# w2 loads issued from ScalarE's queue instead of SyncE's, in a decoder step with a mixture of experts

## The reference

```python
def _moe(x, router_w, router_b, w1, b1, w2, b2):
    logits = x.astype(jnp.float32) @ router_w.astype(jnp.float32) + router_b.astype(jnp.float32)
    top_logits, top_idx = lax.top_k(logits, TOP_K)
    gates = jax.nn.softmax(top_logits, axis=-1)
    combine = jnp.einsum('tk,tke->te', gates,
                         jax.nn.one_hot(top_idx, N_EXPERTS, dtype=jnp.float32)).astype(x.dtype)
    out = jnp.zeros_like(x)
    for e in range(N_EXPERTS):
        a = x @ w1[e] + b1[e]
        glu = jnp.minimum(a[:, ::2], SWIGLU_LIMIT)
        lin = jnp.clip(a[:, 1::2], -SWIGLU_LIMIT, SWIGLU_LIMIT)
        act = glu * jax.nn.sigmoid(SWIGLU_ALPHA * glu) * (lin + 1)
        out = out + combine[:, e:e + 1] * (act @ w2[e] + b2[e])
    return out
```

## Time and profile before

| | |
|---|---|
| median of three runs | 1176.62 us (1175.73 to 1181.22) |
| profiled execution, its own time | 1177.86 us |
| its span, from the first to the last instruction | 1175.8 us |
| granted TensorE clock, mean | 0.977 of full speed |
| TensorE busy | 1081.0 us |
| ScalarE busy | 165.0 us |
| bytes read from HBM | 428.02 MB |

### The profile page before, as it was taken

How to read it: one execution, slowest core, us unless ns; L and a number is a source line. 1 busy time by engine, 2 the same in 40 slices (tenths; PEclk the granted TensorE clock), 3 DMA queues, 4 the chain that set the end, 5 groups by cost and what they waited for, 6 DMA issues and landing times.

```text
span 1175.8 us, 13859 instructions
## 1 busy us (share of the span) xinstructions
PE 1081.0 (92%) x5783; PEld 503.6 (43%) x5783; DVE 293.6 (25%) x490; ACT 165.0 (14%) x339; POOL 62.9 (5%) x103
## 2 busy tenths in 40 slices
PE   6999999899999999898989998989999999898985
PEld 3567774443434343434343434343434343434332
DVE  5338544622213030303030302030303030202022
ACT  3211112402111010101010101010101010101002
POOL 7007001200000000000000000000000000000000
PEclk9999999898999999999999999999999999999998
DMA  9851139289999999999999999999999999999991
GB/s 339 297 215 28 55 145 327 99 343 404 429 427 426 428 427 429 429 428 430 428 429 428 428 429 428 429 428 428 428 430 429 428 428 428 428 428 427 428 416 42
DMA packets 47684, 432.00 MB, mean 367 GB/s; under 512 B 4919, under 2 KB 13655, under 8 KB 22977
## 3 DMA queue, kind: packets, MB, share of 16 engines
q1 hardware_dynamic: 45472, 428.23, 87.3%
q0 software_dynamic: 752, 2.56, 0.7%
q10 hardware_dynamic: 1424, 0.72, 0.2%
HBM read 428.02 MB, written 3.48 MB: 367 GB/s over the span
## 4 chain that ended last, share of the span: by engine, by line
PE 62%; DMA 31%; DVE 2%; ACT 2%; issue 2%; SPq 1%; POOL 0%; ACTq 0%; DVEq 0%; POOLq 0%
DMA ring<-in_expert_w 31%; PE ps L1560 19%; PE ps L1519 13%; PE ps L1476 7%; PE ps L1459 5%; PE ps L1196 5%; PE ps L1180 4%; PE ps L1329 2%; PE ps L1547 1%; PE ps L1246 1%; PE ps L1262 1%; PE ps L1539 1%; PE ps L1282 1%; SPq L369 1%; DMA ring<-in_meta_tokens 0%
## 5 line engine op out<-in xcount | busy, mean ns | idle before, releaser
L1519 PE MATMUL ps<-ring,mem 128*64 128x512 f32 x2048 | 463.7, 609 | 54.7 <-DMA ring<-in_expert_w 54.3
L1519 PEld LDWEIGHTS ps<-ring,mem 128*64 128x64 f32 x2048 | 160.6, 140 | 350.6 <-issue 349.4
L1560 PE MATMUL ps<-ring,mem 128*64 128x512 f32 x1024 | 224.8, 597 | 5.6 <-ACT mem L707 3.0
L1078 DVE TENSOR_SCALAR mem<-ps 128x512 f32<-128x512 f32 x32 | 22.1, 692 | 708.0 <-PE ps L1519 708.0
L1560 PEld LDWEIGHTS ps<-ring,mem 128*64 128x64 f32 x1024 | 86.6, 138 | 133.0 <-issue 133.0
L700 ACT ACTIVATE mem<-mem 128x512 f32<-128x512 f32 x32 | 20.0, 629 | 482.1 <-DVE mem L1078 482.1
L1476 PE MATMUL ps<-mem 128*128 128x512 f32 (+3 forms) x204 | 79.6, 603 | 3.2 <-DVE mem L1080 1.4
L1459 PEld LDWEIGHTS ps<-mem 128*128 128x128 bf16 x1080 | 60.3, 98 | 12.2 <-issue 12.2
L1196 PE MATMUL ps<-mem,ring 128*128 128x280 f32 x256 | 62.9, 401 | 0.9 <-ACT mem L600 0.9
L1459 PE MATMUL ps<-mem 128*128 128x128 bf16 x1080 | 62.9, 219 | 0.0
L1196 PEld LDWEIGHTS ps<-mem,ring 128*128 128x128 f32 x256 | 47.6, 190 | 13.4 <-issue 2.8
(11 more groups left out here) (258 smaller groups left out, 575.5 us busy)
## 6 DMA issues: line engine op xcount, KB each, us to landing
ring<-in_expert_w SPq DMA_DIRECT2D x192, 2048.0 KB, 25.3
ring<-in_w_in SPq DMA_DIRECT2D x7, 2048.0 KB, 19.9
ring<-in_w_out SPq DMA_DIRECT2D x2, 2048.0 KB, 10.1
ring<-in_state_rec SPq DMA_DIRECT2D x4, 512.0 KB, 10.9
out<-ring SPq DMA_DIRECT2D x4, 512.0 KB, 12.6
ring<-in_x_prompt SPq DMA_DIRECT2D x2, 512.0 KB, 4.3
mem<-in_x_prompt POOLq DMA_DIRECT2D x2, 512.0 KB, 6.8
out<-mem SPq DMA_DIRECT2D x2, 512.0 KB
```

The source lines that it names most:

```text
L1078: dve.tensor_scalar(glu[:, at], psA[:, half * D:(half + 1) * D:2], LIMIT, None, ALU.min)\
L1519: done = mm(ps[CAP * e:CAP * e + CAP, b, :], xgT4[:, k, t, CAP * e:CAP * e + CAP], ring[:, slot[e], col:col + HALF], start=False, stop=(t ...
L1560: done = mm(ps[CAP * e:CAP * e + CAP, 4 + half, :], actT3[:, t, CAP * e:CAP * e + CAP], ring[:, slot[e], col:col + HALF], start=(t == 0), ...
```

## The change

The w2 loads leave SyncE's program. ScalarE's `pair` issues them at its head, ahead of its two sigmoids, each with the wait on `w_used` that it had before. SyncE's queue keeps the w1 loads with their waits. Slots, semaphores, sizes and every other instruction stay.

```diff
             def load(k, j, e):
                 slot = (LOADS * k + j) % SLOTS
-                if j < 8:
-                    sp.dma_start(cut(ring[:, slot, :], 2 * D), w1_v[e, j // 2]).then_inc(ring_in[slot], 16)
-                else:
-                    sp.dma_start(cut(ring[:, slot, :], D), w2_v[e, (j - 8) // 2]).then_inc(ring_in[slot], 16)
+                sp.dma_start(cut(ring[:, slot, :], 2 * D), w1_v[e, j // 2]).then_inc(ring_in[slot], 16)
...
             for j in range(7, 8):
                 load(0, j, j % 2)
-            for j in range(8, LOADS):
-                sp.wait_ge(w_used, j - SLOTS + 1)
-                load(0, j, j % 2)
 
             def load_pair(c, i, k, last):
                 n = num(c, i, k)
-                for j in range(LOADS):
+                for j in range(8):
                     sp.wait_ge(w_used, n * LOADS + j - SLOTS + 1)
                     load(k, j, i * 4 + 2 * k + j % 2)
...
             def pair(c, i, k, last):
                 n = num(c, i, k)
+                for j in range(8, LOADS):
+                    slot = (LOADS * k + j) % SLOTS
+                    act.wait_ge(w_used, n * LOADS + j - SLOTS + 1)
+                    act.dma_start(cut(ring[:, slot, :], D), w2_v[i * 4 + 2 * k + j % 2, (j - 8) // 2])\
+                        .then_inc(ring_in[slot], 16)
                 for half in range(2):
                     act.wait_ge(glu_sb, n * 2 + half + 1)
```

## The result

| | before | after |
|---|---|---|
| median | 1176.71 us (4 runs) | 1202.24 us (4 runs) |
| range of the runs | 1175.73 to 1181.22 | 1201.65 to 1205.84 |
| span of the profiled execution | 1175.8 us | 1200.8 us |
| TensorE waiting for w1 | 54.3 us in 28 waits | 66.3 us in 7 waits |
| TensorE waiting for w2 | none | 15.8 us in 4 waits |

The ratio is 1.022, with a 95% interval of 1.0199 to 1.0241: 25.5 us slower, against 23.0 forecast (1199.6, range 1190 to 1209).

A forecast was written before the change was run, and what follows sets the result against it. The prediction took the stream of loads as the bound. Late start 13.7, order 8.3 and clock 1.0 us summed to 23.0, added to a median of 1176.6 for 1199.6 us, range 1190 to 1209.

The forecast's parts named there:

- What bounds the kernel: Whole kernel: the stream of loads is the bound, and TensorE has about 5 us to spare in each pair.
- (1) The issue work: ScalarE's DMA issues: about 1.8 us for four, in steady pairs falling where ScalarE has nothing to do; cost 0.
- (2) The first pair: First pair: w2 issues wait behind the copy of combT until about 265.0, so the stream starts 13.7 us later.
- Difference 0: Hole after the second pair's early w1 loads: about 1 us again, as the 0.9 us before, so nothing added.
- (3) The order of the bytes: Two queues share the engines in halves; in the last pair the last w1 load lands 8.3 us later.
- The steady state: Middle pairs: sharing only shifts which load is waited for; the stream stays full, with at least four slots outstanding.
- (4) The clock: Last w1 step: one longer wait ahead of it makes it slower, 1.0 us, between 0 and 1.7.
- Full penalty: Rival: the order at the end costs 16.6 us, with 13.7 and 1.7 giving 32.0, 1208.6 us; chance 0.14.
- order costs nothing: Rival: queues drained as issued, or ScalarE's behind SyncE's, leaving only 13.7 us, 1190.3 us; chance 0.10.
- no change: Rival: nothing measurable, the stream's late start being hidden, 1176.6 us; chance 0.04.
- A lower rate with two tensors read at once: Rival: 2% less rate while both queues hold loads, some 40% of 900 us, is 7 us; 1207 us; chance 0.07.
- faster: Rival: two queues fill the engines better, needing more than 428 GB/s; 1167 us at 10% more; chance 0.03.

The follow-up runs named there:

- e1: Against the changed kernel: only the first pair's four w2 loads are issued by ScalarE, all others by SyncE; 1192.75 us, ratio 1.0128.
- e4: Against the changed kernel: only the last pair's four w2 loads stay on ScalarE, all others go to SyncE; 1194.9 us, ratio 1.0148.
- e5: On top of e2: in every pair ScalarE waits until w1 load 5 has landed before issuing the w2 loads; 1185.2 us, ratio 1.0071.
- e2: Against the changed kernel: ScalarE issues the first pair's w2 loads ahead of its wait for combT; 1189.15 us, ratio 1.0096.
- e7: Against the changed kernel: the edits of e2 and e5, plus the last two pairs' w2 loads on SyncE; 1178.72 us, ratio 1.0016.

## Why the prediction held, point by point

**What bounds the kernel:** right, and shown. Start the stream late and nothing else, and the whole of it appears in the time (e1: 13.3 us of late start and the 2.5 us of holes that it brings, against 15.4 measured), in spite of TensorE's 5 us of slack in each pair.

**(1) The issue work:** right. ScalarE's four issues of the first pair took 2.12 us against 1.8, ahead of a wait of 14.37 us; in the steady pairs they lie in its idle time (603.73 to 611.52 in the pair from 595.50, whose first sigmoid is at 633.94, behind a wait of 21.04 us).

**(2) The first pair:** the late start was sized 13.7 us and came to 12.1 in the changed kernel's profile, where the mixer happened to be 1.4 us ahead (the gate's exponential at 232.11 instead of 233.51), and 13.3 in e1. The wait at the first w2 product was put at 12 to 15 us and took 14.37. The step "Difference 0" for the hole behind it failed: it is 3.0 us instead of 0.9. The first w2 step was taken at its old length, some 8.4 us, and after the long wait it took 9.48 us, so w1 load 4 was issued at 296 and not at 294.5, while the stream, which had begun earlier, ran dry at about 294.2. The granted clock was 0.50 for most of that step, as in this window of the changed kernel; it had fallen there before the wait, at about 268:

```profile
288.00:290.00 2.00, 2.00 (x6) 0.53 (x4) 0.00 (x0) 0.00 (x0) 0.00 (x0) 0.50 1.02 434
```

**(3) The order of the bytes:** equal shares were right (51.8% and 48.8% in e4). Two things were wrong in it. *The size at the end*, 8.3 us: the changed kernel shows 4.0, e5 6.1 and e4 15.8, the slow steps left out. The term depends on how the last pair is entered. The balance that the prediction relied on does hold, but over two pairs and not over one: a wait of 8.6 to 10.9 us in one pair and none in the next, so the last pair was free of it by its place in the rhythm. The sign that the prediction named for the steady pairs, one wait of 4 to 6 us in each, did not come; the w2 loads did land sooner (22.6 us after their issue in the median, not 26.3), and the stream ended at 1166.8, not near 1160. The two ends that the prediction gave, 0 and 16.6, are about what the runs span. *The steady state*, of which the prediction said that the stream stays full, with at least four slots always outstanding: it does not. While TensorE waits 8.6 us and more for one w1 load, the w2 loads that took the engine time from it land, and with the next w1 loads they fill all eight slots before TensorE frees one. This is 5.3 us between 300 and 1100 us; e2 has 7.4 there, and holding the w2 loads back (e5) closes all but 1.2 of them. The prediction named such holes as what would make it wrong and overrated them: not every pair has one.

**(4) The clock:** 1.0 us was put on the last pair and none was due there, since it has no wait. The slow steps are real (8.70 us after 8.83 us of waiting), but the stream hides them, except in the first pair and where the last w1 step is one of them: 2.55 us in e4, more than the 1.7 allowed, 1.65 in e5 and 1.7 in e7.

Sum as forecast: 13.7 + 8.3 + 1.0 = 23.0. As read from the profile: 12.1 + 8.9 + 4.0 = 25.0. The total was close partly by luck: the start was 1.6 us too large and the terms for order and clock 5.3, and the 8.9 us of holes that were put at nothing filled the place.

**The rivals.** *Full penalty*, *order costs nothing* and *no change* fall with the layout and with e1, e2 and e4. *A lower rate with two tensors read at once* falls too: with both queues busy e4 moves 428 GB/s, and e7 as many bytes as before. The same numbers are against *faster*. The 40% of the time for which both queues were to be busy was low: between 595 and 713 us of the changed kernel both move bytes in 63 of 118 windows of 1 us (each with over 15% of the engines), 53%.

**The rule weighed:** turns of some 9 to 17 descriptors (the Trainium skill, DMA: Bandwidth & Descriptors, "Queues, rings and completion order") would by the prediction's estimate have each engine move a whole load, 4.9 us, from one queue before it turns to the other. Its time of 1201.1 us lies nearer to the measured 1202.24 than the forecast, so the time cannot weigh it; the windows of 0.6 us above can, and they fit a turn after each 16 KB transfer. Here the measurement decides against that size of turn. The same page's statement ("Rules for kernel authors") that several issuing engines bring no bandwidth agrees with e7: 342.57 MB between 300 and 1100 us with two queues as with one.

**What stays open:** about 1 us of the changed kernel's holes is not placed. Of e7's last 2.5 us the slow step is seen in one profile and was not tested. Nor was it tried whether the two-pair rhythm depends on the number of slots.

## What to carry to other kernels

Where the DMA engines are the bound, loads that must arrive in a given order belong in one queue. A second queue halves the rate of whatever is needed first (51.8% and 48.8% of the engines here); in steady state that shows as rarer, longer waits and, with the eight slots of this kernel, as holes, and in the last round it can fall nearly in full on the end (15.8 of 16.6 us in e4). And a load inherits every wait that stands ahead of it in the issuing engine's program: read the first round of the loop apart, since what stands in front there is not what stands in front later.

## What was not expected of the hardware

The time of one pair went to a rhythm of two: from 423 us to the last pair, 63.9 to 65.7 us and 53.0 to 54.5 us in turn, where the pairs from 396 us on took 57.0 to 60.6 us before, from equal work and equal loads. And the turn between two queues seems to be a single 16 KB packet of 0.61 us on each engine, with nine engines in one phase and seven in the other: that is how the counts of 9 and 7 in successive windows of 0.6 us are read here.
